# A streaming encoder layer on one core: the third block's down projection in seven products, with sums of its weights made by GpSimd one block earlier

## The reference

```python
def merge_and_ffn(x, attn, conv, g, w_out, g_post_mix, g_pre_ffn, w_ffn_gate, w_ffn_up, w_ffn_down, g_post_ffn):
    m = g[:, :, 0] * attn + g[:, :, 1] * conv
    x = x + rmsnorm(m @ w_out, g_post_mix)
    h = rmsnorm(x, g_pre_ffn)
    f = (jax.nn.silu(h @ w_ffn_gate) * (h @ w_ffn_up)) @ w_ffn_down
    return x + rmsnorm(f, g_post_ffn)
```

## Time and profile before

| | |
|---|---|
| three runs | 2985.45, 2989.43, 2993.73 us, median 2989.43 |
| the profiled execution | 2988.57 us, its span 2986.8 us |
| granted TensorE clock, mean | 0.997 of full speed |
| TensorE busy | 2932.4 us, 98% of the span |
| VectorE, ScalarE, GpSimd busy | 2030.7, 1451.5, 680.0 us |

### The profile page before, as it was taken

One profiled execution on the slowest core, in us unless ns is written; L12 is line 12 of the kernel. 1 busy time (PEld: TensorE's weight loads), 2 busy tenths in 40 slices (PEclk: granted clock), 3 DMA queues, 4 the chain that ended last, 5 costly groups with the idle time before them and its releaser, 6 DMA issues. The chain is left out here.

```text
span 2986.8 us, 50911 instructions
## 1 busy us (share of the span) xinstructions
PE 2932.4 (98%) x18791; PEld 2618.2 (88%) x18791; DVE 2030.7 (68%) x3674; ACT 1451.5 (49%) x2877; POOL 680.0 (23%) x658
## 2 busy tenths in 40 slices
PE   8999999999999999999999999999999999999998
PEld 7777789988888889998888888999899999899976
DVE  8998779874797747663398775665369867466623
ACT  5766555554455535553155544554225554455412
POOL 4950035520581000000086000000039400100001
PEclk9999999999999999999999999999999999999999
DMA  8875746678654355556655444556565443445543
GB/s 297 274 244 200 268 146 210 206 280 300 223 190 166 128 187 166 179 182 226 218 195 185 142 156 158 188 186 210 196 208 173 169 132 121 170 157 172 178 168 122
DMA packets 204454, 573.44 MB, mean 192 GB/s; under 512 B 24000, under 2 KB 26816, under 8 KB 203696
## 3 DMA queue, kind: packets, MB, share of 16 engines
q1 hardware_dynamic: 191728, 548.81, 54.2%
q10 hardware_dynamic: 12480, 21.38, 1.9%
HBM read 456.03 MB, written 114.16 MB: 191 GB/s over the span
## 5 line engine op out<-in xcount | busy, mean ns | idle before, releaser
L1325 PE MATMUL PS<-h_hi,w_hi 128*128 128x512 f32 (+2 forms) x1664 | 533.4, 353 | 9.0 <-DVE u L2710 5.4
L1325 PE MATMUL PS<-h_hi,w_lo 128*128 128x512 f32 (+2 forms) x1664 | 525.3, 349 | 0.0
L1325 PE MATMUL PS<-h_lo,w_hi 128*128 128x512 f32 (+2 forms) x1664 | 525.3, 348 | 0.0
L1355 PE MATMUL PS<-op_hi,w_hi 128*128 128x256 f32 x1680 | 476.6, 284 | 2.2 <-DVE w_lo L2429 2.2
L1355 PE MATMUL PS<-op_lo,w_hi 128*128 128x256 f32 x1680 | 475.4, 283 | 0.0
L1355 PE MATMUL PS<-op_hi,w_lo 128*128 128x256 f32 x1680 | 475.4, 283 | 0.0
L1221 POOL TENSOR_TENSOR y<-y,prod 128x512 f32<-128x512 f32 (+1 forms) x333 | 431.8, 1325 | 157.9 <-ACT prod L1947 144.9
L2314 DVE SCALAR_TENSOR_TENSOR PS<-u,dw,PS 128x512 f32<-128x512 f32 (+1 forms) x604 | 434.1, 766 | 7.0
L2429 DVE TENSOR_TENSOR w_lo<-raw,w_hi 128x512 fp32r<-128x512 f32 x376 | 287.8, 775 | 155.1 <-ACT w_hi L1799 154.3
L1325 PEld LDWEIGHTS PS<-h_hi,w_hi 128*128 128x128 f32 x1664 | 293.9, 188 | 53.3 <-issue 13.1
L1325 PEld LDWEIGHTS PS<-h_hi,w_lo 128*128 128x128 f32 x1664 | 294.0, 188 | 39.3
(11 more groups left out here) (316 smaller groups left out, 5864.0 us busy)
## 6 DMA issues: line engine op xcount, KB each, us to landing
w_lo<-lo_dram SPq DMA_DIRECT2D x240, 512.0 KB, 4.5
w_hi<-hi_dram SPq DMA_DIRECT2D x240, 512.0 KB, 3.6
raw<-in_w_stream SPq DMA_DIRECT2D x292, 256.0 KB, 3.4
w_raw<-sum_dram SPq DMA_DIRECT2D x180, 256.0 KB, 3.0
w_raw<-in_w_stream SPq DMA_DIRECT2D x80, 512.0 KB, 5.2
hi_dram<-w_hi SPq DMA_DIRECT2D x80, 512.0 KB, 5.6
lo_dram<-w_lo SPq DMA_DIRECT2D x80, 512.0 KB, 3.7
sum_dram<-raw ACTq DMA_DIRECT2D x60, 256.0 KB, 2.3
```

What stands on the lines that cost most here:

```text
L1325: last = nc.tensor.matmul(PS[:, k0 + off, col:col + n], w, x[:, k, c0:c0 + n], start=first and k == 0, stop=stop and k == KT - 1)
L1355: last = nc.tensor.matmul(out, w[:, part_k], o[:, k, :], start=start and first and k == 0, stop=stop and k == KH - 1, skip_group_check=again)
```

## The change

In the third block (`SEVEN = (2,)`) the down projection is done in seven products too. The 22 row tiles of `f` are 11 pairs e (even and odd tile), the frames two halves of 256, the weights two rows by two halves of the columns. A piece (i, e) is product i's share of pair e: 256 frames by 128 rows by 512 columns, two tiles of 128 frames, three matmuls each. There are 77 pieces in the order `DOWN`: products 1 and 5 in turns, 2 and 6, 4 and 7, then 3. Products 1, 6 and 7 run on in the same two banks of PSUM (`X2`); what they hold is copied out by ScalarE after each (`hold`), and VectorE adds five times 128x1024 to `third` and `held`, which become the results of the tiles 0, 1 and 2, 3. Products 1, 2 and 3 (`KEPT`) take plain weights, 256 KB of high and 256 KB of low part; products 4 to 7 take sums of weights, 256 KB from `t_dram`, which ScalarE and VectorE split anew for each piece. The sums of `f` are made by GpSimd, nine pieces ahead. The next block's norm has its transposes after the pieces 7, 14, 21, 28 and 35, and uses two banks of its own.

The sums of weights are made by GpSimd in the second block (`MAKES_T = 1`), in 22 halves of a pair's columns: two loads of 256 KB from the weights' stream, four subtractions of 128x256 in place, a store of 512 KB, all issued on GpSimd's queue. Three halves (`EARLY_T`) use one place and stand ahead of the second block's `post_inv_rms` of its out projection; the other 19 use three places during gate and up. ScalarE's copy of f tile 19's first product (`j == FT - 3`) waits for the stores of the first two places, since these lie in the last tiles of `f`; SP waits for all stores before it loads the next block's rows. Semaphores that are renamed or shared by the diff keep their waits.

```diff
+SEVEN = (2,)
+MAKES_T = 1
+KEPT = (1, 2, 3)
+X2, Z2, Y2, W2 = 2, 4, 6, 0
+def passes():
+    order = []
+    for lead, other in ((1, 5), (2, 6), (4, 7)):
+        order += [(lead, 0), (lead, 1)]
+        for e in range(HALF_D - 2):
+            order += [(lead, e + 2), (other, e)]
+        order += [(other, HALF_D - 2), (other, HALF_D - 1)]
+    return order + [(3, e) for e in range(HALF_D)]
+FR = 6
+DAHEAD = 4
+WAHEAD = 3
+SUM_AHEAD = 9
+S0_AT = [2 + 7 * tt for tt in range(5)]
+EARLY_T = 3
+T_PLACE = [2] * EARLY_T + [h % 3 for h in range(2 * HALF_D - EARLY_T)]
...
+            def load_of_sums(h):
+                if h >= 2 * HALF_D:
+                    return
+                n = T_PLACE[h]
+                if t_uses(h) > 1:
+                    pool.wait_ge(t_out[n], 16 * (t_uses(h) - 1))
+                elif n < 2:
+                    pool.wait_ge(op_ok, len(OPS) * (MAKES_T + 1))
+                else:
+                    pool.wait_ge(w_used, G(MAKES_T, S_W) + 1)
+                    pool.wait_ge(pv_done, U0[MAKES_T] + units(MAKES_T))
+                    pool.wait_ge(o_read, U0[MAKES_T] // 2 + outputs(MAKES_T))
+                cols_of = slice(h % 2 * T // 2, (h % 2 + 1) * T // 2)
+                for half in range(2):
+                    src = w_stream[S_D + 2 * FT + half * HALF_D + h // 2].rearrange("p (k n) -> p k n", k=2)
+                    pool.dma_start(t_sum[n][:, half], src[:, :, cols_of]).then_inc(t_in[n], 16)
+            def sums_of_weights(first, end, ahead):
+                for h in range(first, min(first + ahead, end)):
+                    load_of_sums(h)
+                for h in range(first, end):
+                    n, made = T_PLACE[h], len(SUMS) * NP + 4 * h
+                    b11, b21, b12, b22 = (t_sum[n][:, half, odd, :] for half in range(2) for odd in range(2))
+                    pool.wait_ge(t_in[n], 32 * t_uses(h))
+                    nc.gpsimd.tensor_tensor(b11, b12, b11, ALU.subtract).then_inc(ws_ok, 1)
...
+                    pool.wait_ge(ws_ok, made + 4)
+                    pool.dma_start(t_dram[h // 2, h % 2], t_sum[n][:]).then_inc(t_out[n], 16)
+                    if h + ahead < end:
+                        load_of_sums(h + ahead)
...
                     if s == S_F - 1:
+                        if b == MAKES_T:
+                            sums_of_weights(0, EARLY_T, 1)
                         post_inv_rms(b, 0, 0)
...
+                        if b == MAKES_T:
+                            sums_of_weights(EARLY_T, 2 * HALF_D, 3)
...
+            def down_of_seven(b):
+                for v, (i, e) in enumerate(DOWN):
+                    if i in KEPT:
+                        down_landed(pe, b, v)
+                    else:
+                        pe.wait_ge(weight_low_ok, 1 + raw_units(b, v))
+                    low_piece_made(pe, b, v)
+                    k = {1: X2, 6: X2, 7: X2, 5: Z2, 2: Y2, 3: Y2, 4: W2}[i]
...
+                    hi, lo = down_high(v), down_low(v)
+                    for t in range(2):
+                        x_hi, x_lo = (d[:, v % FR, t * P:(t + 1) * P] for d in (d_hi, d_lo))
+                        for x, w, start, stop in ((x_hi, hi, True, False), (x_hi, lo, False, False),
+                                                  (x_lo, hi, False, True)):
+                            last = nc.tensor.matmul(PS[:, k + t, :], x, w, start=start and e == 0 and i not in (6, 7),
+                                                    stop=stop and e == HALF_D - 1, skip_group_check=i in (6, 7))
...
+                    if b == MAKES_T and j == FT - 3:
+                        for n in range(2):
+                            act.wait_ge(t_out[n], 16 * T_PLACE.count(n))
                     finished(act, b, (j, 1))
                     A(f[:, j, N1:T], PS[:, bank_of(j, 1), 0:N1], ACT.Copy).then_inc(copied, 1)
...
+                        elif i == 3:
+                            down_used(dve, b, v)
+                            TT(held[:], two_banks(Y2), held[:], ALU.add).then_inc(c_ok, 1)
...
+                    if v == DSLOT[3, 8]:
+                        residual(b, 0, 1)
+                        residual(b, 1, 1)
...
-                for tt in range(4):
+                for tt in range(2 if seven(b) else 0, 4):
                     residual(b, tt, 1)
```

More of the change, by code:

```diff
@@ L360, in ext, with seven, plain_before, sevens_before @@
             return b == NB - 1
+        def seven(b):
+            return b in SEVEN
+        def plain_before(b):
+            return sum(not seven(bb) for bb in range(b))
+        def sevens_before(b):
+            return sum(seven(bb) for bb in range(b))
         def tiles(b):
@@ L412, in out_tile, with down_tile @@
             return sum(tiles(bb) - 1 for bb in range(b)) + tt + 1
+        def down_tile(b, tt):
+            return sum(tiles(bb) - 1 for bb in range(b) if not seven(bb)) + tt + 1
         def post_tile(b, tt, second):
@@ L620, in neighbours @@
         def neighbours(b, tt, second):
+            if second and seven(b):
+                return False
             kept = tt < 2 and stash_of(b, second) is not None
@@ L628, in stashes @@
         def stashes(b, second):
-            return 2 * b + 2 * ext(b) * second + 2
+            return 2 * plain_before(b) + 2 * ext(b) * second + 2
         def o_half(b, half, tt, second):
+            if second and seven(b):
+                if tt < 2:
+                    return PS[:, Z2 + tt, :] if half else third[:, tt, :]
+                return (held if half else stash_of(b, second))[:, tt - 2, :]
             if half == 0 and tt < 2 and stash_of(b, second) is not None:
@@ L639, in pair @@
             if not second:
+                if b and seven(b - 1):
+                    return W2, W2 + 1
                 k = 4 + 2 * (tt % 2) if b or tt != 2 else 2
@@ L758, in lo_made, with loaded_later, turned_before @@
             eng.wait_ge(w_lo_ok, g + 1)
-        def first_in(ring, slot):
-            return NS + (slot - NS) % ring
+        def loaded_later(g):
+            return g >= NS and not (seven(g // NS) and g % NS >= S_D)
         def nth(g, ring):
-            return (g - first_in(ring, g % ring)) // ring + 1
+            return sum(loaded_later(gg) for gg in range(g % ring, g + 1, ring))
+        def turned_before(eng, b, tt):
+            if b and seven(b - 1):
+                if tt:
+                    eng.wait_ge(hf_ok, first_norm(b, tt))
+            elif b and tt >= 2:
+                eng.wait_ge(hf_ok, first_norm(b, tt) - 1)
@@ new lines, in down_high, with down_low, down_raw, down_landings @@
+        def down_high(v):
+            return w_hi[:, (S_F - 4 + PLACE[v] // 2) % HI, PLACE[v] % 2 * HW:(PLACE[v] % 2 + 1) * HW]
+        def down_low(v):
+            return w_lo[:, (S_F - 5 + PLACE[v] // 2) % LO, PLACE[v] % 2 * HW:(PLACE[v] % 2 + 1) * HW]
+        def down_raw(v):
+            return w_raw[:, (S_F - 5 + PLACE[v] // 2) % LO, PLACE[v] % 2 * HW:(PLACE[v] % 2 + 1) * HW]
+        def down_landings(k, end):
+            return sum(2 if DOWN[u][0] in KEPT else 1 for u in range(end) if PLACE[u] == k)
@@ new lines, in place_free, with raw_units, low_piece_made @@
+        def place_free(eng, b, v):
+            before = [u for u in range(v) if PLACE[u] == PLACE[v]]
+            if before:
+                down_used(eng, b, before[-1])
+            else:
+                unit_used(eng, b, NU - 8 + PLACE[v])
+        def raw_units(b, v):
+            per = sum(i not in KEPT for i, _ in DOWN)
+            return per * sevens_before(b) + sum(i not in KEPT for i, _ in DOWN[:v + 1])
+        def low_piece_made(eng, b, v):
+            eng.wait_ge(flo_ok, pieces_before(b) + v + 1)
@@ L769, in s0_at, with two_banks, tile_at @@
+        def two_banks(k):
+            return PS[:, k:k + 2, :]
+        def tile_at(b, v, after):
+            at = S0_AT[:tiles(b + 1)]
+            return at.index(v - after) if v - after in at else None
         def s0_at(s, b):
@@ L1198, in _, with sums_for @@
+            def sums_for(b, first, end):
+                for v in range(first, min(end, ND7)):
+                    if DOWN[v] in SUM_POS:
+                        sum_of_pieces(b, *DOWN[v])
             nc.gpsimd.memset(neghalf, -0.5).then_inc(setup_ok, 1)
@@ L1291, in transpose_tile @@
                 scaled(pe, n)
-                if not second and b and tt >= 2:
-                    pe.wait_ge(hf_ok, first_norm(b, tt) - 1)
+                if not second:
+                    turned_before(pe, b, tt)
+                if not second and b and seven(b - 1) and tt == 0:
+                    for bank in range(W2, W2 + 2):
+                        out_made(pe, b - 1, *last_read(bank))
                 if not second and b == 0 and tt == 3:
@@ new lines, in high_of_sum, with hold @@
+            def high_of_sum(b, v):
+                if v < ND7 and DOWN[v][0] not in KEPT:
+                    down_landed(act, b, v)
+                    place_free(act, b, v)
```

(11 more changed lines are left out.)

275 lines of the change are left out of this document (243 added, 32 removed).

## The result

The changed kernel took 3024.54 us (median of 4 runs, 3022.30 to 3036.35), the kernel before 2988.30 beside it (4 runs). The ratio is 1.0127, with a 95% interval of 1.0097 to 1.0157: 36 us slower, where -7 was forecast with a range that ended at 2997. The profiled execution took 3024.49 us and spans 3022.7, 35.9 more than before.

A forecast was written before the change was run, and what follows sets the result against it. TensorE, busy 98% of the span, was taken as the bound. -14.96 + 1.7 + 5.7 + 0.5 + 0 = -7.1 us on the profiled run's 2988.57 gave 2981.5 us, with a range of 2975 to 2997.

The forecast's parts named there:

- What bounds the kernel: Whole kernel: TensorE busy 98% of the span, so a microsecond less of its work is a microsecond of time.
- The down, -14.96: Third block's down projection: 66 fewer matmuls at 0.2267 us save 14.96 us, with all other work hidden beside TensorE.
- Rival D: Third block's down not bound by TensorE: GpSimd's sums slow VectorE, stage some 116 us, +7, 2988.5 us; chance 0.11.
- The end, +1.7: End of third block's down: fourth block's second step +3.0, a later wait shrinks by 1.3; net +1.7 us (0 to 4).
- The three early halves, +5.7: Second block's out projection: three halves of weight sums ahead of GpSimd's inverse root delay TensorE's gate and up, 5.7 us.
- F: Time when GpSimd is free of the three early halves: 1077.2 + 3L + 9.6 + 2S, taken as 1108.0.
- L and S: Times of an early half's two loads (L, taken as 4.2 us) and of its store (S, 4.3 us).
- rival B: Second block's early halves nearly free: GpSimd done by 1105 and weights in time, 2976 to 2979 us; chance 0.21.
- The late halves, 0: Second block's gate and up: the 19 later halves end at 1311.8, 5 us to spare before ScalarE's copy; no cost.
- rival C: Second block's gate and up: late halves delay ScalarE's copy if c exceeds 8.58; 2989 us at c = 9; chance 0.22.
- the cycle c: GpSimd's time per cycle in the late halves: sums 3.2 to 3.6, store 4.0, issues 0.8, about 8.3 us.
- Contention in gate and up, +0.5: Second block's gate and up: VectorE's 84 low halves slowed beside GpSimd, 24 us at most, mostly in free time; +0.5.

The follow-up runs named there:

- no_f_sums: all_late with the sums of f left out, the pieces using plain f (output not the reference's): 2982.04 us, ratio to before 0.9970.
- seven_only: Changed kernel without making sums of weights, plain weights of the same size standing in (output not the reference's): 2987.97 us, ratio to before 0.9994.
- all_late: Changed kernel with GpSimd's store-waiting load issued one half later and the three early halves moved into gate and up: 2988.88 us, ratio 1.0002.
- paced_early_norm: all_late with product 7's sums of f earlier, product 3's one per two pieces, next norm's first two tiles two pieces earlier: 2980.41 us.
- its twin: paced_early_norm, with the fourth block's second step waiting only for PSUM readers and the state loaded ahead of y's store: 2977.01 us.

## Why the prediction was wrong, point by point

**What bounds the kernel: right, and not used to the end.** TensorE has nothing to spare, so the waits that GpSimd caused were time. The prediction named the queue positions that mattered, and mis-sized what stood in them. Of the 43 us between forecast and result (3024.5 for 2981.5) the down is 12.8, the early halves 11.9, the late ones 18.9, the end 0.4; the rest came out 1.0 better. The prediction also let no term come from the clock, since it saw no long gaps for TensorE. The gaps came, and behind them the clock was near half: some 1.0 us after the early wait (17.7 us from the inverse root on, for 16.7, if that is all clock), 1.6 after the late one (18.9 less 17.25 of waiting) and 1.7 in the down (5 us at 0.66), some 4 of the 43.

**The down, -14.96: the count was right, the cover was not.** 462 matmuls were issued, but the stage gave 2.2 us and not 15. The step that failed is the one that put 83 of 109 us on VectorE and called it cover. It is an average over four phases. In three of the four a pair of pieces needs at most one weight sum split; in products 4 and 7 both do, which makes 2.1 us of VectorE's work (two splits, two low halves of `f`) for 2.72 us of TensorE's, and there GpSimd, unpaced, made 25 sums on end, with 1.16 us instead of 0.69 for each split and 0.62 for a low half: 3.6 us, more than TensorE needs. Rival D had the mechanism, with 0.11, and set against it that GpSimd's sums lie beside a third of VectorE's work: a third, but this third. no_f_sums puts the contention at 6.8 us by the medians and 9.6 by the ratios, the lower clock behind the waits included. The other part wasn't named: the norm's rows were loaded only four pieces before they are used, ScalarE stood 3.28 us for them with the pieces' high parts behind it, and TensorE's clock dropped after that. This is read from the trace; no run shows what it is worth by itself. I had noted the DMA's share as room; a load's lateness isn't seen in a share.

**The end, +1.7:** +2.8 at the second step (predicted +3.0), and 0.7 given back after it of the 1.3 expected; 2.1 in all, right.

**The three early halves, +5.7: right in mechanism, a third of the size.** The step that failed is F, 1108.0 for 1118.95; from F to gate and up it took 17.7 us for 16.7, some of it at the lower clock. L and S came from medians over the whole program (3.4, 3.7 to 5.6 us) and from an upper bound of 6, though the earlier trace rows showed the DMA at 0.99 at the start of this stretch: there the first pair of loads took 8.5 us and the first store 7.6. Of the 10.95 us the loads are 5.5, the stores 2.2, the later start 1.9, sums and the last issue 1.3. The Trainium skill, "DMA: Bandwidth & Descriptors", section "Anatomy of one DMA — SWDGE (gpsimd) path", has a fit for one transfer, about 2.0 us and its bytes over 436 GB/s; by it 256 KB take 2.6 and 512 KB 3.2, an estimate. The trace shows some two and a half times that where the DMA's share was 1.02 (8.5 for two loads of 256 KB, 7.6 for the store), and 3.2 for the second store, which lay in 1107 to 1119, with a share of 0.24. The prediction's rival B, near to that price, fell. The prediction's 1103 takes 3.2 for the pair of loads (2.6 gives 1101), and not all rows were at or above the fit, as it says: ScalarE's store of 256 KB took 2.3.

**The late halves, 0: rival C, with 0.22, is what happened.** The step that failed is the cycle c, 8.3 for 10.05. The price list was short in two of its three items: sums 4.1 us for 3.2 to 3.6, since each subtraction was longer beside VectorE (0.72 alone, 0.9 to 1.0 on average); issues 2.0 us for 0.8, since a load's issue takes GpSimd 0.72 us (1.44 for the pair) and the store's 0.57; the rest 3.9, about the 4.0 assumed. Together 10.05 for 8.3, past the limit of 8.58. For c = 10 the prediction's time was 3007, some 25 us for this; it was 18.9, mainly because the last two halves, whose loads had long been issued, took some 4 us each (1341.80, 1345.85) where 18c counts 10. The late halves alone put the forecast at 3000, beyond 2997, a case that the prediction saw and left out of its range; that early halves and cover failed with them made it 3024.5, and no rival had them fail together.

**Contention in gate and up, +0.5:** no run shows it apart; seven_only and all_late differ by 0.9 us with and without all sums there, so it is small. Its bound of 24 us was read from 84 low halves; the same stretch has 60 more of the same length (689 ns), which makes it 41. The Trainium skill's rule that a VectorE instruction with two SBUF inputs contends with a GpSimd one that reads SBUF ("SBUF — State Buffer", "Who interferes with whom") agrees with the traces: VectorE went from 688 to 1164 ns in the down and to 915 in gate and up of all_late, GpSimd from 0.72 to 1.07 us a subtraction.

Still open: which of the remaining waits in paced_early_norm (3.2 us) comes from what, why its twin's profile had one of 2.65, and 2.8 of the down's 12.8 us, which are neither in its waits (8.3) nor in the clock (1.7).

## What to carry to other kernels

A wait for a transfer belongs as far behind its issue as the places allow: the same 22 halves took 10.05 us each when GpSimd waited for the store it had just issued and 6.60 when it did one half's work in between. Check cover phase by phase and in the phase where two demands meet, not over a stage; and price a transfer by the rows of the stretch in which it will run. If an idle engine is given work, see first what stands behind it in its queue.

## What the runs showed of the hardware

A DMA issue on GpSimd took 0.72 us for a load of 256 KB in 1 KB runs and 0.57 for a store of 512 KB, and in the timeline GpSimd does nothing else in that time. On SP's queue most issues of the changed kernel in 1165 to 1214 took 0.32 to 0.46 us, a few up to 1.38. Waits of TensorE of 2.2 to 2.7 us were followed in several runs by a stretch at the 1.2 GHz level, and so cost more than themselves (2.19 us at 2129.53 of the changed kernel, then 5 us at 0.66). It isn't the same each time: after 2.20 us at 2092.21 in no_f_sums the granted clock stayed at 1.00 (2092 to 2096), and after the wait before the fourth block's second step, 2.6 us in the changed kernel and 2.7 in all_late, the granted clock was 1.00 in the one (2227 to 2233) and 0.79 in the other (2198 to 2206).
